# VectorE's low parts and takes, each as one operation, in a three-term fp32r decoder layer

## The reference

```python
D_MODEL, SEQ, D_FF = 2048, 256, 5504

def swiglu(h, w_gate, w_up, w_down):
    return (jax.nn.silu(h @ w_gate) * (h @ w_up)) @ w_down

h = rmsnorm(x, ffn1_norm[l])
x = x + 0.5 * swiglu(h, ffn1_w_gate[l], ffn1_w_up[l], ffn1_w_down[l])
...   # projection, two groups, output projection, cross attention
h = rmsnorm(x, ffn2_norm[l])
x = x + 0.5 * swiglu(h, ffn2_w_gate[l], ffn2_w_up[l], ffn2_w_down[l])
```

## Time and profile before

| | |
|---|---|
| median of 3 runs | 1888.04 us |
| the profiled execution | 1887.78 us, span 1886.0 us from its first to its last instruction |
| TensorE (PE) | 1877.8 us busy, 8836 matmuls |
| VectorE (DVE) | 1550.6 us, 82%, 1955 instructions |
| ScalarE (ACT) | 1078.0 us, 57% |
| TensorE's granted clock | full speed in all 40 slices |
| DMA engines | 57.1% for the queue that loads the weights |

### The profile page before, as it was taken

The page is one execution under the profiler, slowest core; times in us unless marked ns, Lnnn a source line. Parts: engine busy times, 40 slices in busy tenths (PEclk is TensorE's granted clock), DMA queues, the critical chain, the costliest instruction groups (busy, mean ns, idle before and its releaser), DMA issues.

```text
span 1886.0 us, 23078 instructions
## 1 busy us (share of the span) xinstructions
PE 1877.8 (100%) x8836; PEld 1576.7 (84%) x8836; DVE 1550.6 (82%) x1955; ACT 1078.0 (57%) x1437; POOL 96.5 (5%) x98
## 2 busy tenths in 40 slices
PE   9999999999999999999999999999999999999999
PEld 8888888888889888988888888888888888888987
DVE  6999998979999867655666774689999978899986
ACT  7665555555656547545476655656565554555553
POOL 0000000000000001312260000000000000000000
PEclk9999999999999999999999999999999999999999
DMA  9656565656556665555443554456656665655655
GB/s 337 223 196 200 187 221 181 228 194 201 180 184 219 212 226 156 168 179 179 136 155 112 202 190 144 156 179 200 201 181 205 217 221 174 208 194 184 198 191 171
DMA packets 177294, 362.55 MB, mean 192 GB/s; under 512 B 8096, under 2 KB 19360, under 8 KB 176544
## 3 DMA queue, kind: packets, MB, share of 16 engines
q1 hardware_dynamic: 176896, 360.89, 57.1%
q10 hardware_dynamic: 288, 0.19, 0.0%
HBM read 358.95 MB, written 2.10 MB: 191 GB/s over the span
## 4 chain that ended last, share of the span: by engine, by line
PE 96%; DVE 1%; ACT 1%; POOL 1%; DMA 1%; issue 0%; SPq 0%; DVEq 0%; ACTq 0%; POOLq 0%
PE acc L1904 19%; PE acc L1903 19%; PE acc L1902 19%; PE acc L1891 8%; PE acc L1893 8%; PE acc L1892 8%; PE small L1902 2%; PE small L1904 2%; PE small L1903 2%; PE small L2102 2%; PE tr L1853 1%; PE tr L1904 1%; PE tr L1902 1%; PE tr L1903 1%; PE tr L1918 1%; DMA w_raw<-in_ffn_w_gate 1%
## 5 line engine op out<-in xcount | busy, mean ns | idle before, releaser
L1269 DVE TENSOR_TENSOR w_lo<-w_raw,w_hi 128x1024 fp32r<-128x1024 f32 (+2 forms) x720 | 724.6, 1060 | 66.6 <-ACT w_hi L709 47.0
L709 ACT ACTIVATE w_hi<-w_raw 128x1024 fp32r<-128x1024 f32 (+4 forms) x552 | 513.9, 963 | 168.9 <-PE acc L1904 124.4
L1902 PE MATMUL acc<-w_hi,hT_hi 128*128 128x512 f32 (+1 forms) x920 | 354.8, 386 | 0.0
L1904 PE MATMUL acc<-w_lo,hT_hi 128*128 128x512 f32 (+1 forms) x920 | 353.2, 384 | 0.0
L1903 PE MATMUL acc<-w_hi,hT_lo 128*128 128x512 f32 (+1 forms) x920 | 353.0, 384 | 0.0
L1198 DVE TENSOR_TENSOR w_lo<-w_raw,w_hi 128x1024 fp32r<-128x1024 f32 (+1 forms) x184 | 218.1, 1225 | 58.9 <-ACT w_hi L709 57.4
L803 ACT ACTIVATE w_hi<-w_raw 128x1024 fp32r<-128x1024 f32 (+1 forms) x176 | 182.3, 1044 | 112.1 <-DVE w_raw L1257 60.2
L1902 PE MATMUL acc<-w_hi,actT_hi 128*128 128x512 f32 x548 | 213.9, 390 | 0.0
L1904 PE MATMUL acc<-w_lo,actT_hi 128*128 128x512 f32 x548 | 213.3, 389 | 0.0
L1903 PE MATMUL acc<-w_hi,actT_lo 128*128 128x512 f32 x548 | 213.2, 389 | 0.0
L1904 PEld LDWEIGHTS acc<-w_lo,hT_hi 128*128 128x128 f32 x920 | 172.7, 188 | 32.5
(11 more groups left out here) (306 smaller groups left out, 2549.2 us busy)
## 6 DMA issues: line engine op xcount, KB each, us to landing
w_raw<-in_ffn_w_down SPq DMA_DIRECT2D x68, 1024.0 KB, 5.2
w_raw<-in_w_in SPq DMA_DIRECT2D x36, 1024.0 KB, 5.1
w_raw<-in_ffn_w_gate SPq DMA_DIRECT2D x38, 768.0 KB, 4.3
w_raw<-in_ffn_w_up SPq DMA_DIRECT2D x38, 768.0 KB, 4.4
w_raw<-in_ffn_w_gate SPq DMA_DIRECT2D x56, 512.0 KB, 3.9
w_raw<-in_ffn_w_up SPq DMA_DIRECT2D x54, 512.0 KB, 4.8
w_raw<-in_ffn_w_up SPq DMA_DIRECT2D x26, 1024.0 KB, 5.8
w_raw<-in_ffn_w_gate SPq DMA_DIRECT2D x24, 1024.0 KB, 5.0
```

The lines of the kernel that those rows point to most:

```text
L709: nc.scalar.activation(piece(w_hi, c % SPLIT, k0, k1, width), piece(raw, c % RAW, k0, k1, width), ACT.Copy).then_inc(hi_done, 1)
L1269: v.tensor_tensor(piece(w_lo, c % RAW, k0, k1, width), piece(raw, c % RAW, k0, k1, width), piece(w_hi, c % SPLIT, k0, k1, width).bitcast(F ...
L1902: mm(dst, lhs_hi, wh, start=first, stop=False)
L1904: return mm(dst, lhs_hi, wl, start=False, stop=last)
```

## The change

1. VectorE's low parts of a plain slot become one operation over all its tiles (`lo_whole`). It waits for both high parts and raises `lo_done` by 2.
2. The low parts of a raw slot become one operation over three tiles (`lo_raw`). For that the four tiles are loaded in another order, so that the tile TensorE doesn't use stands first: two loads, one to the tiles 1 and 2, one to the tiles 0 and 3. In down duos these were one load of two tiles of 1024 columns. The sum of tiles 1 changes its sign, and so does the token sum that it is multiplied with.
3. `take_first` and `take_second` take both token tiles in one operation. `first_taken` and `second_taken` are raised by 2 at once.
4. Made slots keep their two low parts, and ScalarE keeps two high parts for each slot.

```diff
-PLAIN_PARTS = {n: halves(n) for n in range(2, 5)}
-RAW_PARTS = ((0, 1), (2, 4))
+RAW_PARTS = ((1, 2), (2, 4))
...
-                fetches[r], fetches[r + 1] = 2 if duo.up else 1, 0
+                fetches[r], fetches[r + 1] = 2, 0
...
+                        sp.dma_start(tiles[:, 1:3, 0:d.width], rows_of(wl, k0, 2, slice(n0, n0 + d.width))).then_inc(loaded[c % RAW], 16)
+                        sp.dma_start(tiles[:, 0:4:3, 0:d.width], rows_of(wr, k0, 2, slice(n1, n1 + d.width))).then_inc(loaded[c % RAW], 16)
...
-                done(v.tensor_tensor(rest[1], src[:, 0, 0:P], src[:, 0, P:SEQ], ALU.subtract))
+                done(v.tensor_tensor(rest[1], src[:, 0, P:SEQ], src[:, 0, 0:P], ALU.subtract))
...
-                v.tensor_tensor(made[:, 0:2, :], b[:, 1:4:2, :], b[:, 0:2, :], ALU.subtract).then_inc(ev("combined"), 1)
+                v.tensor_tensor(made[:, 0:2, :], b[:, 0:1, :].broadcast_to([P, 2, width]), b[:, 1:4:2, :], ALU.subtract).then_inc(ev("combined"), 1)
...
-            def lo_parts(c, parts, width, unit=None):
-
-                for i, (k0, k1) in enumerate(parts):
-                    if unit is not None and i == 1:
-                        dve.wait_ge(ev("combined"), 2 * unit + 2)
+            def lo_whole(c, k0, k1, width):
+
+                dve.wait_ge(hi_done, 2 * c + 2)
+                v.tensor_tensor(piece(w_lo, c % RAW, k0, k1, width), piece(raw, c % RAW, k0, k1, width),
+                                piece(w_hi, c % SPLIT, k0, k1, width).bitcast(F32), ALU.subtract).then_inc(lo_done, 2)
+
+            def lo_raw(c, n, width):
+
+                dve.wait_ge(ev("combined"), 2 * n + 2)
+                lo_whole(c, 1, 4, width)
+
+            def lo_made(c, width):
+
+                for i, (k0, k1) in enumerate(MADE_PARTS):
...
-                for t in range(TT):
-                    if d.up:
-                        w = d.width
-                        dve.wait_ge(ev("parts_taken"), m + 1)
-                        v.tensor_tensor(gate[:, t, 0:w], acc[:, GB[d.f], t, 0:w], gate[:, t, 0:w], ALU.add).then_inc(ev("first_taken"), 1)
+                if d.up:
+                    w = d.width
+                    dve.wait_ge(ev("parts_taken"), m + 1)
+                    v.tensor_tensor(gate[:, :, 0:w], acc[:, GB[d.f], :, 0:w], gate[:, :, 0:w], ALU.add).then_inc(ev("first_taken"), TT)
...
-                product(P1, *A11, c, 0, w, first, last).then_inc(slot_used, 1)
+                product(P1, *A11, c, 1, w, first, last).then_inc(slot_used, 1)
```

More of the change, by code:

```diff
@@ L482, in load_unit @@
                         sp.wait_ge(slot_used, 2 * (c - RAW + 1))
+                        tiles = raw[:, c % RAW, :].rearrange("p (k n) -> p k n", k=4)
                         if d.up:
[L484 to L487, removed]
-                        else:
-                            dst = raw[:, c % RAW, :].rearrange("p (k n) -> p k n", k=2)
-                            sp.dma_start(dst, rows_of(wd, f0 + k, 2, slice(2 * d.block * NW, 2 * (d.block + 1) * NW))).then_inc(loaded[c % RAW], 16)
+                            n0 = n1 = (f0 + 4 * d.block) * P
+                            k0, wl, wr = k, wg, wu
+                        else:
+                            n0, n1 = 2 * d.block * NW, (2 * d.block + 1) * NW
+                            k0, wl, wr = f0 + k, wd, wd
+                        sp.dma_start(tiles[:, 1:3, 0:d.width], rows_of(wl, k0, 2, slice(n0, n0 + d.width))).then_inc(loaded[c % RAW], 16)
+                        sp.dma_start(tiles[:, 0:4:3, 0:d.width], rows_of(wr, k0, 2, slice(n1, n1 + d.width))).then_inc(loaded[c % RAW], 16)
                     def load_plain(c, side, k, tiles):
@@ L1284, in take_second @@
                 dve.wait_ge(slot_used, 2 * d.end)
-                for t in range(TT):
-                    if d.up:
-                        w = d.width
-                        dve.wait_ge(ev("parts_taken"), m + 1)
[L1289 to L1292, removed]
+                if d.up:
+                    w = d.width
+                    dve.wait_ge(ev("parts_taken"), m + 1)
+                    v.tensor_tensor(nat[:, :, 0:w], acc[:, 1 - GB[d.f], :, 0:w], nat[:, :, 0:w], ALU.add).then_inc(ev("second_taken"), TT)
+                else:
+                    at_ = slice((2 * d.block + 1) * NW, (2 * d.block + 2) * NW)
+                    v.scalar_tensor_tensor(x[:, :, at_], acc[:, 1 - GB[d.f], :, :], 0.5, x[:, :, at_], ALU.mult, ALU.add).then_inc(ev("second_taken"), TT)
             def multiply_up(m):
@@ L1306, in take_first @@
                 dve.wait_ge(slot_used, 2 * (d.firsts[-1] + 1))
[L1307 to L1310, removed]
-                        v.tensor_tensor(gate[:, t, 0:w], acc[:, GB[d.f], t, 0:w], gate[:, t, 0:w], ALU.add).then_inc(ev("first_taken"), 1)
-                    else:
-                        at_ = slice(2 * d.block * NW, (2 * d.block + 1) * NW)
-                        v.scalar_tensor_tensor(x[:, t, at_], acc[:, GB[d.f], t, :], 0.5, x[:, t, at_], ALU.mult, ALU.add).then_inc(ev("first_taken"), 1)
+                if d.up:
+                    w = d.width
+                    dve.wait_ge(ev("parts_taken"), m + 1)
+                    v.tensor_tensor(gate[:, :, 0:w], acc[:, GB[d.f], :, 0:w], gate[:, :, 0:w], ALU.add).then_inc(ev("first_taken"), TT)
+                else:
+                    at_ = slice(2 * d.block * NW, (2 * d.block + 1) * NW)
+                    v.scalar_tensor_tensor(x[:, :, at_], acc[:, GB[d.f], :, :], 0.5, x[:, :, at_], ALU.mult, ALU.add).then_inc(ev("first_taken"), TT)
             def take_parts(m):
@@ L1342, in duos @@
                 combine(DUOS[m0].raws[0], v0, NW)
-                lo_parts(DUOS[m0].raws[0], RAW_PARTS, NW, v0)
-                lo_parts(DUOS[m0].raws[0] + 1, MADE_PARTS, NW)
+                lo_raw(DUOS[m0].raws[0], v0, NW)
+                lo_made(DUOS[m0].raws[0] + 1, NW)
                 for m in range(m0, LAST[f] + 1):
@@ L1363, in duos @@
                             combine(d.raws[n], u0 + n, w)
-                            lo_parts(d.raws[n], RAW_PARTS, w, u0 + n)
+                            lo_raw(d.raws[n], u0 + n, w)
                             if n == 1 and turns_in(d):
                                 turn_round_lo(m, 0)
-                            lo_parts(d.raws[n] + 1, MADE_PARTS, w)
-                        lo_parts(d.firsts[n], PLAIN_PARTS[tiles], w)
+                            lo_made(d.raws[n] + 1, w)
+                        lo_whole(d.firsts[n], 0, d.plains[n][1], w)
                         if n == 0 and m > m0 and DUOS[m - 1].up:
@@ L1379, in duos @@
                             take_first(m)
-                        lo_parts(d.seconds[n], PLAIN_PARTS[tiles], w)
+                        lo_whole(d.seconds[n], 0, d.plains[n][1], w)
                         if n == 0 and u1 == len(d.plains):
@@ L1389, in duos @@
                             token_sums(actT_sum[:, 2 * n, P:SEQ], [aS_sum[:, n, i, :] for i in range(3)], flat[n % 3])
-                        lo_parts(e.raws[0], RAW_PARTS, e.width, u0 + u1)
+                        lo_raw(e.raws[0], u0 + u1, e.width)
                         for n in new_sums(m):
@@ L1393, in duos @@
                                                         (actT_lo[:, 2 * n, P:SEQ], actT_sum[:, 2 * n, P:SEQ], actT_hi[:, 2 * n, P:SEQ])])
-                        lo_parts(e.raws[0] + 1, MADE_PARTS, e.width)
+                        lo_made(e.raws[0] + 1, e.width)
             def first_pair(f):
```

## The result

The changed kernel takes **1902.82 us** (median of 4 runs, 1902.54 to 1903.9), the kernel before 1888.1 us beside it (4 runs, 1887.77 to 1888.45): ratio 1.0079, 95% interval 1.0067 to 1.0092, 14.7 us slower. The forecast was 1894.7 with a range of 1890.0 to 1899.0: the direction is as forecast and so are most of the places, the size is more than twice as large and outside the range. TensorE's granted clock is full in both profiles.

What follows compares the result with a forecast made beforehand. TensorE, busy 1877.8 of 1886.0 us, was taken as the bound; its added lateness behind VectorE's longer round in four halves summed 2.87 + 1.14 + 1.54 + 1.14 = 6.7 us, giving 1894.7, range 1890.0 to 1899.0.

Steps and rivals of the forecast that it cites:

- VectorE's round: VectorE's time from take to take in up duos: 42.41 - 0.60 + 0.98 = 42.79 us, 0.34 longer than TensorE's.
- the round trip: Up duos, first accumulator's take through ScalarE's Silu and high parts to the third seconds slot's low part and next sums: +0.98 us.
- H: VectorE's lateness behind the round trip in up duos: 0.81 us in duo 14, growing by 0.38 a duo without waits.
- rival C: TensorE also waits at units' raw slots in some 14 of 20 up duos: about +5, 1899.7 us; chance 0.10.
- nine duos that have no wait left: Bound where fusing saves 0: 0.67 us more in each of these duos, 1900.7 us in all.
- Its first stretch: Feed-forward 1, first half: 2.25 us by duo 2, duos 3 and 4 add 0.3 each, given as 2.87.
- 0.067 us a fusion: VectorE: two operations of 1024 take 2.35 us, a single one of 2048 would take 2.283.
- its two terms: Up duos: Silu starts 0.54 us later behind the whole take; the low part 0.52 later behind both high parts.
- the slots at which TensorE waits: PE waits on w_lo in duos 2 to 4, 9 to 12, 15 to 18, 23 to 26, some 0.3 us each.
- no cost of the down duos' 512 KB loads: Down duos: two 512 KB loads land after 4.8 us each, with over 8 us to spare: cost 0.
- no cost of the order: A unit's new tile order (broadcast operand, negated factor) keeps element counts: cost 0, within 0.1 us a unit.
- VectorE's busy time: Whole program: 272 + 55 fusions x 0.067 us make VectorE's busy time about 22 us less.

Runs made afterwards that it cites:

- e_wait: The kernel before, with the low part of a raw slot's first tile also waiting for the unit's last sum, nothing fused: 1889.7 us.
- a_rawhalves: The changed kernel with the raw slots' low parts in two operations again, the first behind the first sum only: 1900.03 us.
- e_order: The kernel before with the new order of a unit's tiles alone (loads, broadcast operand, sign), nothing fused: 1888.4 us.

## Why the prediction was wrong

- **The step that failed** is VectorE's round, "42.41 - 0.60 + 0.98 = 42.79 us, 0.34 longer than TensorE's". It is 43.22, 0.77 longer. Missing is the raw low part's wait for the last sum, +0.35, a cost that the prediction put at nothing (shown by e_wait in kind, by after and a_rawhalves in size: from 43.22 to 43.05, where the split also gives back the 3 x 0.067 that fusing had saved). The other 0.07 to 0.08 are in the round trip: net +1.05, not 0.98. That the raw slot's low part waits for the sums as well stands among the rows of the order; the prediction priced it nowhere. Its price stood in the trace of before: a sum that waits for the one in front (L1259 to L1261) starts 0.73 us after it, an operation that doesn't wait for it 0.61 us (the first three of the five rows of before above).
- **How many duos count** was the second error in size. The sum let VectorE's waits swallow most of H, its lateness, at duos 1, 9, 11, 15, 23 and 25, and rival C reckoned further lateness in "nine duos that have no wait left". By that count 0.43 more of a round would be 3.9 us and the forecast 1898.6. The measured slope is 15 to 16 duos of 20: duo 15 added 0.93 instead of 0.30, duo 25 0.81 instead of 0. A wait takes away a fixed amount once; beyond it each further us is exposed. (Its first stretch, 2.25 and twice 0.3, adds up to 2.85 and not 2.87; nothing hangs on that.)
- **Rival C's mechanism** took part: TensorE waits at the third unit's raw slot as well (duo 15, in the rows below: 0.52 from start to start instead of 0.23, and then 0.34). This wait isn't in the table of waits at all. Its 1899.7 lacked the longer round. It was not a case beside the forecast but the same one, further on.
- **Right**: 0.067 us a fusion (2287 ns); the round trip as the main cost, and its two terms but for 0.08; the slots at which TensorE waits; no cost of the down duos' 512 KB loads, which land as forecast (second fence below), and delay there only in the first down duo of a second half, though more than the sum had (duo 26 0.58 instead of 0.30); no cost of the order (e_order).
- **VectorE's busy time** fell by 15.1 us, not by 22. Busy time is the union of the records, so overlap counts once. A low part that used to overlap the last 0.08 us of its sum now starts behind it, at 74 of the 88 raw slots, 6.1 of the missing 7 us. e_wait shows it alone: with that wait and the same 1955 instructions VectorE is busy 6.2 us longer (1550.6 before; the row of e_wait is in the third fence below).
- **The Trainium skill**: "VectorE: DVE Perf Modes", in its section on the DRAIN, says that a semaphore between two operations of the engine costs nothing extra, and its rules for kernel authors say to minimize the count of operations, not the semaphores. The runs here differ. e_wait adds one such wait per raw slot, and the operation behind it starts 0.12 us later. 327 operations fewer save VectorE's work, 0.067 us each, and yet the program is 14.7 us slower. The measurement decides.

Timeline of TensorE after, duo 15, the first product of the third unit's raw slot:

```profile
1313.31 0.39 PE L1911 MATMUL acc<-w_lo,hT_hi 128*128 128x512 f32 x1
1313.83 0.50 PE L1909 MATMUL small<-w_hi,hT_hi 128*128 128x512 f32 x1
1314.17 0.39 PE L1910 MATMUL small<-w_hi,hT_lo 128*128 128x512 f32 x1
```

DMA issues after (count, KB each, us from issue to landing), beside the earlier trace rows:

```profile
w_raw<-in_ffn_w_down SPq DMA_DIRECT2D x56, 512.0 KB, 4.8
```

Page of e_wait, part 1:

```profile
PE 1880.6 (100%) x8836; PEld 1576.6 (83%) x8836; DVE 1556.8 (82%) x1955; ACT 1074.0 (57%) x1437; POOL 95.4 (5%) x98
```

## What to carry to other kernels

Before fusing two operations of a producer, write down for each half what it waited for and who waited for it: the fused one inherits the latest input and the latest output. The 0.067 us saved stand against 0.54 to 0.60 us for each handover on a chain and 0.12 to 0.18 us for each new wait on the engine's own last result. Where two engines run rounds of equal length, compare rounds, not busy shares: 0.77 us beyond the bound engine's round was paid in some 15 of 20 rounds.

## What the hardware showed

- Behind an operation of 512 elements on VectorE one that waits for it starts after 0.73 to 0.79 us, another after 0.61.
- TensorE needs 0.12 us to be back in step after each wait (0.79 us for the next three starts instead of 0.68), besides the wait itself. The prediction had 0.13, though its row showed 0.33 instead of 0.23 for the next start alone.
- The table of waits showed 5.4 us on feed-forward low parts where 14.7 were lost; only start times against the other kernel's show it.
